# Twelve context projection units and the context norm moved into the convolution stage, all convolution taps on VectorE

## The reference, cut to what matters

```python
# first layer of the first block
u = h @ w_in + b_in                      # 1024 -> 2048
u = u[..., :D] * sigmoid(u[..., D:])     # GLU
u = causal_dwconv(u, dw, dw_b)           # depthwise, 31 taps over positions
u = silu(layer_norm(u, ln_g, ln_b))
y = u @ w_out + b_out

# second block: x is the stream, ctx a second input of 256 positions
mod  = silu(c)     @ ada_w + ada_b       # 6 x 1024, shift and scale of the stream
modc = silu(c_ctx) @ ada_w + ada_b       # only its shift sh1c and scale sc1c are used
u  = modulate(rmsnorm(x,   norm1_g), sh1,  sc1)
uc = modulate(rmsnorm(ctx, norm1_g), sh1c, sc1c)
pl, pc = split(u @ w_in_2), split(uc @ w_in_2)
# of pc: keys, values, gates of the mLSTM, keys and values of the diff attention
```

## Time and profile before

| what | value |
|---|---|
| median of 3 runs | 2381.61 us (2378.51 to 2382.83) |
| span of the profiled execution | 2380.3 us (it has no other time of its own) |
| mean granted TensorE clock | 0.994 |
| PE busy | 2316.2 us, 97% |
| DVE busy, ACT busy | 769.2 us, 423.7 us |
| DMA | 611.40 MB, 65% of the 16 engines' span |

### The profile page before, as it was taken

The page is one execution under the profiler, slowest core; times in us unless marked ns, Lnnn a source line. Parts: engine busy times, 40 slices in busy tenths (PEclk is TensorE's granted clock), DMA queues, the critical chain, the costliest instruction groups (busy, mean ns, idle before and its releaser), DMA issues.

```text
span 2380.3 us, 31802 instructions
## 1 busy us (share of the span) xinstructions
PE 2316.2 (97%) x13124; PEld 1756.2 (74%) x13124; DVE 769.2 (32%) x1881; ACT 423.7 (18%) x1035; POOL 0.2 (0%) x4
## 2 busy tenths in 40 slices
PE   9999999999999999999999999999999999998998
PEld 7888888888888888888887787555555555554555
DVE  7834374210435421100355823222222222221222
ACT  4332102010242211100024402111111111111111
POOL 0000000000000000000000000000000000000000
PEclk9999999999999999999999999999999999999999
DMA  7134476655324444234332377999999999999997
GB/s 268 40 138 157 145 291 238 230 214 192 107 89 142 155 146 142 71 123 134 86 120 87 140 276 287 404 426 427 429 427 428 427 428 427 429 427 427 427 427 297
DMA packets 61048, 611.40 MB, mean 257 GB/s; under 512 B 7016, under 2 KB 8424, under 8 KB 10896
## 3 DMA queue, kind: packets, MB, share of 16 engines
q1 hardware_dynamic: 60944, 609.93, 65.1%
HBM read 606.74 MB, written 1.06 MB: 255 GB/s over the span
## 4 chain that ended last, share of the span: by engine, by line
PE 81%; DMA 10%; DVE 7%; issue 1%; ACT 0%; DVEq 0%; SPq 0%; ACTq 0%
PE bank L645 28%; PE bank L1197 16%; PE bank L642 8%; DMA ring<-in_experts 6%; PE bank L1234 5%; PE bank L733 5%; DMA arena<-in_experts 4%; PE bank L659 3%; DVE arena L1868 3%; PE bank L634 2%; PE bank L1188 2%; PE bank L1156 1%; PE bank L1144 1%; PE bank L744 1%; PE bank L764 1%
## 5 line engine op out<-in xcount | busy, mean ns | idle before, releaser
L645 PE MATMUL bank<-arena,ring 128*128 128x256 f32 x3264 | 709.9, 380 | 0.0
L645 PEld LDWEIGHTS bank<-arena,ring 128*128 128x128 f32 x3264 | 620.8, 190 | 84.4
L2300 DVE TENSOR_SCALAR arena<-bank 128x256 f32<-128x256 f32 x64 | 27.1, 424 | 673.9 <-PE bank L1197 673.9
L1197 PE MATMUL bank<-ring,arena 128*64 128x256 f32 x2048 | 235.2, 384 | 9.0 <-DMA ring<-in_experts 6.7
L1197 PE MATMUL bank<-arena 128*64 128x256 f32 x2048 | 231.5, 380 | 10.5 <-DMA arena<-in_experts 10.3
L1197 PEld LDWEIGHTS bank<-ring,arena 128*64 128x64 f32 x2048 | 143.6, 138 | 115.6 <-issue 33.3
L1197 PEld LDWEIGHTS bank<-arena 128*64 128x64 f32 x2048 | 144.9, 137 | 98.6 <-DMA arena<-in_experts 17.2
L642 PE MATMUL bank<-ring,arena 128*128 128x256 f32 x896 | 194.0, 379 | 1.0 <-issue 1.0
L642 PEld LDWEIGHTS bank<-ring,arena 128*128 128x128 f32 x896 | 170.1, 190 | 24.4 <-issue 1.4
L733 PE MATMUL bank<-arena,ring 128*128 128x256 f32 x576 | 124.6, 379 | 0.0
L1625 ACT ACTIVATE arena<-arena 128x256 f32<-128x256 f32 x64 | 26.7, 416 | 533.9 <-DVE arena L2300 533.9
(11 more groups left out here) (306 smaller groups left out, 1907.5 us busy)
## 6 DMA issues: line engine op xcount, KB each, us to landing
arena<-in_experts SPq DMA_DIRECT2D x96, 2048.0 KB, 31.1
ring<-in_dense SPq DMA_DIRECT2D x185, 1024.0 KB, 4.9
ring<-in_experts SPq DMA_DIRECT2D x87, 2048.0 KB, 29.5
ring<-in_experts SPq DMA_DIRECT2D x16, 1024.0 KB, 31.4
ring<-arena SPq DMA_DIRECT2D x16, 128.0 KB, 5.8
con<-in_con SPq DMA_DIRECT2D x1, 1248.0 KB, 12.2
X<-in_x SPq DMA_DIRECT2D x2, 512.0 KB, 5.8
ring<-in_dense SPq DMA_DIRECT2D x2, 512.0 KB, 7.4
```

Source lines behind the costliest of these rows:

```text
L645: ins = nc.tensor.matmul(o, w[:, k, j * P:(j + 1) * P], src[:, k, :], start=(k == 0), stop=(k == KT - 1))
L1197: ins = nc.tensor.matmul(o, XGT[:, k, e * CAP:(e + 1) * CAP], w[:, k, :], start=False, stop=(k == KT - 1), skip_group_check=True)
```

## The change

- A stage `early` of 12 slabs and 12 units stands between `cm_in` and `cm_out`. Its slabs are copies of those of mv, dv and dk: each is now read twice, once for the context and once for the stream.
- The context norm and its modulation (eight slabs, read again for it into places of their own) run beside `cm_in`, on DVE in the middle of `conv(0)`.
- The results, and the normed context, are written to DRAM (`park`, 4 x 1 MB) and fetched back before `ffn1_in` slab 1 and before dk.
- All 31 taps of all eight tiles are on DVE; the diagonal matrices are gone, and the filler matmuls ahead of `cm_out`, in whose place half an early unit stands.
- mv, dk and dv have four units each; the wait for the read-out of dk is gone.

The core of the diff, cut:

```diff
-    ("cm_in", 8, 8), ("cm_out", 4, 4),
+    ("cm_in", 8, 8), ("early", EARLY, EARLY), ("cm_out", 4, 4),
...
-    ("mk", 2, 4), ("mq", 2, 2), ("mv", 4, 8),
-    ("dq", 4, 4), ("dk", 4, 8), ("dv", 4, 8),
+    ("mk", 2, 4), ("mq", 2, 2), ("mv", 4, 4),
+    ("dq", 4, 4), ("dk", 4, 4), ("dv", 4, 4),
...  (SP, ahead of slab g)
+                    sp.dma_start(CT, d_ctx).then_inc(sem("ctx_in"), 16)                       # g == 2
+                    sp.dma_start(CSR[:, 1, :], d_cond[:, D:2 * D]).then_inc(sem("ctx_in"), 16)
+                for i in ((), (0, 1), (2,), (3, 4), (5,), (6, 7))[g - 2] if 2 <= g < 8 else ():
+                    if i >= CTX_PLACES:
+                        sp.wait_ge(sem("ada_ctx"), 2 * (i - CTX_PLACES) + 2)
+                    sp.dma_start(ADA_C[i % CTX_PLACES], d_dense[SLAB_AT["ada", i]])...
+                if g == SLAB_AT["early", 0] + RING + 1:
+                    sp.wait_ge(sem("nc_h"), before("nc_h") + KT)
+                    park(3, UC)
+                for b in range(3):
+                    if g == SLAB_AT["early", 0] + 4 * b + 4 + RING:
+                        for u in range(3):
+                            unit_half(sp, FIRST_UNIT["early"] + 4 * b + 1 + u, 2)
+                        park(b, STAGED[b])
                 if g == SLAB_AT["ffn1_in", 1]:
                     sp.wait_ge(sem("att_out"), HEADS)
-                    sp.dma_start(CT, d_ctx).then_inc(sem("ctx_in"), 16)
+                    sp.wait_ge(sem("parked"), 4 * 16)
+                    sp.dma_start(UC, tiles(d_park[3], KT)).then_inc(sem("parked_back"), 16)
+                    sp.dma_start(DV[:, 0:2, :], tiles(d_park[1], 2)).then_inc(sem("parked_back"), 16)
+                    sp.dma_start(DK[:, :, 0:T], tiles(d_park[2], KT)).then_inc(sem("parked_back"), 16)
...  (PE)
-            conv_taps(5, banks[WORK + 3][:, 0:T], TAPS - PE_TAPS, 0)
-            conv_taps(6, banks[WORK + 1][:, 0:T], 0, PE_TAPS)
+            pe.wait_ge(sem("nc_h"), before("nc_h") + KT)
+            for n in range(7):
+                early(n)
             for c in range(4):
                 channel_sum(c)
-            conv_taps(7, banks[WORK + 2][:, 0:T], 0, PE_TAPS + TAPS)
-            for c in range(4, KT):
+            for n in range(7, EARLY - 2):
+                early(n)
+            for c in range(4, 6):
+                channel_sum(c)
+            early(EARLY - 2)
+            early(EARLY - 1, (0,))
+            for c in range(6, KT):
                 ins = channel_sum(c)
             ins.then_inc(sem("ln_mean"), 1)
             stat("ln", 1, mean)
-            stage("cm_out", H, "ln_h", busy=6)
+            early(EARLY - 1, (1,))
+            stage("cm_out", H, "ln_h")
...
-            units_read(pe, "dk")
             pe.wait_ge(sem("rt"), 1)
-            for i in range(8):
-                product(FIRST_UNIT["dv"] + i, SLAB_AT["dv", i // 2], (UC, H)[i % 2], True)
+            stage("dv", H, token_major=True)
...  (ACT)
             root("n0", 0)
+            act.wait_ge(sem("ctx_in"), 32)
+            nc.scalar.activation(CSR[:, 1, :], CSR[:, 1, :], ACT.Silu).then_inc(sem("silu_ctx_done_by_act"), 1)
+            square("nc", lambda c: CT[:, c, :])
             act.wait_ge(sem("par_in"), 16)
             for j in range(8):
+                if j == 3:
+                    root("nc", 1)
+                if j == 7:
+                    shifted("nc", 1, 0, UC)
...  (DVE)
+            def context():
+                dve.wait_ge(sem("ada_ctx"), 2 * CTX_ADA)
+                gains(1)
+                modulated("nc", rstd("nc", 1), CT, lambda c: GS1[:, c, 1:2], UC)
...
             raw_unit(0)
             normed("n0", factor, lambda c: ("mix_pre", c))
+            presum("nc")
             dve.wait_ge(sem("par_in"), 16)
             glu(0)
             raw_unit(1)
             glu(1)
-            conv(0)
+            beside = {k + 1: [(ada_ctx, (k,))] for k in range(CTX_ADA)}
+            beside[CTX_ADA + 2] = [(context, ())]
+            conv(0, beside)
             glu(2)
             glu(3)
-            conv(2, between={4: (4, 5), 14: (6,), 22: (7,)})
-            conv(4, own=(TAPS, TAPS - PE_TAPS))
-            dve.wait_ge(sem("conv_pe"), 1)
-            V.tensor_tensor(U[:, 5, :], U[:, 5, :], banks[WORK + 3][:, 0:T], ALU.add).then_inc(sem("conv"), 1)
+            conv(2, {4: [(glu, (4,)), (glu, (5,))], 14: [(glu, (6,))], 22: [(glu, (7,))]})
+            conv(4)
+            conv(6)
```

More of the change, by code:

```diff
@@ L460, in build, with early_to @@
                 if name in ("mq", "dq"):
[L461 to L468, removed]
+                    dst = [to[:, 2 * i + j, :] for j in range(2)]
+                elif name == "dk":
+                    dst = [to[:, 2 * i + j, T:2 * T] for j in range(2)]
+                else:
+                    dst = [to[:, 2 + j, i * T:(i + 1) * T] for j in range(2)]
+                second.append((FIRST_UNIT[name] + i, dst))
+        def early_to(n, j):
+            b, i = n // 4, n % 4
+            if b < 2:
+                return tiles(STAGED[b], 2)[:, j, i * T:(i + 1) * T]
+            return tiles(STAGED[b], KT)[:, 2 * i + j, :]
         def kvq(i, j):
@@ L841, in _ @@
             stage("cm_in", XG, first=1, count=1)
[L842 to L851, removed]
+            stage("cm_in", H, "n0_h", first=2, count=1)
@@ L853, in channel_sum @@
+            presummed("nc")
+            stage("cm_in", H, first=3, count=5)
             def channel_sum(c):
[L855 to L858, removed]
+                pe.wait_ge(sem("conv"), c + 1)
                 return nc.tensor.matmul(banks[WORK][:, 0:T], mean, U[:, c, :], start=(c == 0), stop=(c == KT - 1))
-            conv_taps(5, banks[WORK + 3][:, 0:T], TAPS - PE_TAPS, 0)
@@ L862, in _, with early @@
-            conv_taps(6, banks[WORK + 1][:, 0:T], 0, PE_TAPS)
+            def early(n, halves=(0, 1)):
+                u, g = FIRST_UNIT["early"] + n, SLAB_AT["early", n]
+                w = slab(g).rearrange("p (k n) -> p k n", k=KT)
+                if halves[0] == 0:
+                    slab_loaded(pe, g)
+                    unit_half(pe, u - UNIT_BANKS, 2)
+                for j in halves:
+                    for k in range(KT):
+                        if n < 8:
+                            ins = nc.tensor.matmul(half_of(u, j), UC[:, k, j * P:(j + 1) * P], w[:, k, :],
+                                                   start=(k == 0), stop=(k == KT - 1))
+                        else:
+                            ins = nc.tensor.matmul(half_of(u, j), w[:, k, j * P:(j + 1) * P], UC[:, k, :],
+                                                   start=(k == 0), stop=(k == KT - 1))
+                if halves[-1]:
+                    ins.then_inc(sem(f"unit{u % UNIT_BANKS}"), 1)
@@ L890, in _ @@
             presummed("n7")
-            stage("ffn1_in", H, first=1, count=10)
-            presummed("nc", 0)
-            stage("ffn1_in", H, first=11, count=11)
+            stage("ffn1_in", H, first=1, count=21)
             ffn_out(1, "n8")
[L896 to L903, removed]
+            pe.wait_ge(sem("parked_back"), 48)
             product(FIRST_UNIT["mk"], SLAB_AT["mk", 0], UC)
@@ L926, in _ @@
             ins.then_inc(sem("cumf_turn"), 1)
-            two("mv", True)
+            stage("mv", H, token_major=True)
             pe.wait_ge(sem("gate_steps"), 3)
@@ L1466, in _ @@
             root("n7", 1)
[L1467 to L1486 removed]
+            ffn_in(1)
             root_table("n8")
@@ L2359 @@
     }
+    weights["early"] = np.concatenate([weights["mv"], weights["dv"], weights["dk"]])
     for i in range(2):
```

168 lines of the change are left out of this document (82 added, 86 removed).

## The result

| | us |
|---|---|
| changed kernel, median of 4 runs | 2353.36 (2351.0 to 2356.95) |
| kernel before, beside it | 2381.86 (2378.51 to 2382.83) |
| ratio | 0.9882, 95% interval 0.987 to 0.9894 |
| profiled execution: own time, span | 2351.0, 2349.2 |

The account below looks back on a forecast made before the run. TensorE was taken as the bound, with VectorE setting the convolution stage and the weight stream the experts. Terms 51.2 - 83.0 - 0.4 - 1.0 + 1.5 = -31.7 us took span 2380.3 to 2348.6, time 2350; range 2343 to 2362.

Parts of the forecast that it names:

- (a) to (c): VectorE's chain in the convolution stage: conv starts at 29.1, conv(0) ends at 76.8, the last tap at 152.2 us.
- (a): VectorE before the first tap: the presum of context squares ahead of glu(0) makes conv start 2.7 us later.
- (f): DMA: 28 MB more, with modulation slabs queued behind waits, parking and fetches, all priced as free.
- (d): TensorE in the convolution stage: idles 3.7 us before sum 6; cm_out starts at 160.9, 51.2 us later.
- (g): TensorE's clock falls to half after the new idle in the convolution stage: +1.5 us, bounds 0 and 4.
- (e): mLSTM projections: -83.0, -0.4 and -1.0 us; k's rotation keeps about 5 us of cover, any excess paid one for one.
- The first: Convolution stage fully VectorE-bound and longer than priced: up to 12 us more, about 2362; chance 0.12.
- The second: mLSTM stage: k's turn and rotation end after dv, m_scores waits 3 to 15 us, say 2358; chance 0.08.
- The third: Convolution stage PE-bound, DVE ending by 148: no idle or clock fall, 5.2 us less, 2345; chance 0.07.
- Slab supply: Slabs of mv, dk and dv arrive slower than PE takes them: 33 us lost, or even 2409; chance 0.03.
- the unmoved expert stream: Expert stage at the end: its weight stream starts by something that does not move, nothing gained, 2381; chance 0.03.

Follow-up runs that it names:

- e0: The changed kernel itself, run once more without any edit: 2353.99 us.
- e2: Changed kernel with the modulation products three taps later in conv(0) and the context norm at tap 13 instead of 10: 2354.08 us.
- e1: Changed kernel with 13 filler matmuls on TensorE in the idle before channel sums 6 and 7: 2351.99 us.
- e5: Changed kernel with the 32 narrow gate matmuls placed two by two behind wide matmuls of the last mk unit, instead of in a block: 2349.84 us.
- e9: Changed kernel with 30 idle VectorE operations inside the rotation of k, holding it up by 13.7 us: 2361.69 us.
- e4: Changed kernel with later modulation products, the context squares' adds spread between taps, and the first tap of tiles 2 to 7 on ScalarE: 2351.0 us.
- e8: Changed kernel with the first eight taps of channel tiles 6 and 7 given back to TensorE: 2353.4 us.
- e3: Kernel before with only the tap part of the change, all taps on VectorE and context work as before: 2411.61 us.
- e6: Changed kernel with the wait for the read-out of all dk units put back ahead of dv: 2356.64 us, a single time.
- e7: Changed kernel with the edits of e4 and e5 together, plus three filler matmuls before channel sums 6 and 7: 2342.83 us.

## Why the prediction was right

- *Where the gain is.* Cm_out later by 55.3, the mLSTM projections shorter by 84.6, the expert stage earlier with them. 2353.36 beside the forecast 2350, within the range.
- *(a) to (c), VectorE's chain.* The last tap but one ended at 153.1 for 151.8. That this is so near is in part luck, as two errors cancel. Conv started at 27.25, not 29.1: 1.4 us of it because this execution's head was earlier (in e0, with a later head, 29.26), and 0.4 because (a) was priced too long. And the taps lost 2.7 us to the slabs of (f). The context norm took 5.4 us, tap pairs 24.4, as priced, and without the slab waits, in e2, the stretch from the first tap to sum 6 is 123.2 us, where the prediction has 122.7.
- *(f), the step that was wrong in kind:* I had the modulation slabs land 2.5 us ahead of their use. The sixth and seventh came late by 0.7 and 1.8: issued at 33.4 and 36.5, behind what was already on a queue that moved 418 to 424 GB/s, they could not be used before 44.1 and 49.1, 10.7 and 12.6 us later. The conclusion "free" fell, the price (1.1 to 2.7, e2) was inside the range.
- *(d), the idle.* 6.2 us for 3.7: PE was 1.2 us earlier (146.9 for 148.1), DVE 1.3 later.
- *(g), the clock:* the mechanism right, the term mis-sized: +1.5 forecast, 2.55 by e1 and 4.0 in e0. The Trainium skill, "TensorE: Matmul & The Clock Gate", Part 1 with its section on HAM oscillation, says that an idle gap drops the clock to half and that sustained work brings it back. The windows at 150 (0.50) and 160 (1.00) and e1 agree. What I missed is a second place: the block of narrow gate matmuls, where PE is busy and the clock falls all the same. It was there in the kernel before, which I had not looked at. By the stretch that e5 shortens it costs 3.3 to 6.6 us, depending on the execution.
- *(e), the cover behind dv.* The rotation ended 4.0 us before dv for "about 5". That the excess past this point would be paid one for one is refuted by e9: the read-out behind it decides, later.
- *Rivals.* The first (a longer DVE chain) came in part, by the slabs, under 3 us. The second did not come. The third is what e4 and e8 reach only by edits. Slab supply and the unmoved expert stream are refuted by the first gate half and the end moving 29 to 31 us.
- *The span is 31.1 us shorter, the stages above give 29.3.* 1.4 of the rest is one fall of the clock at 1340 that this execution did not have after the same idle; e1, e3, e4, e5, e6 and e7 had it, e0, e2, e8 and e9 not. 0.4 is behind it, in the gates and experts, and stays open. So does the rest of the spread from 2351 to 2357: other executions than the profiled one have no trace. That the span comes within 0.6 us of the forecast is in part luck: this execution is the fastest of the four, its head is 1.4 us earlier than that of the kernel before, and it lacks the fall at 1340. The span of e0, the same code, is 27.8 us shorter than before.

## What to carry to other kernels

Where two engines share a stage, work given to the bound one is paid in full (e3), and work put on the idle one beside it is free up to the point where their ends meet (e4, e8): write down both sequences to their ends before moving either. Fill what idle remains, or the clock takes part of the gain back (e1), and look for narrow matmuls in blocks: a busy engine can stand at half clock (e0), and mixing them between wide ones saved 4.1 us here (e5).

## What the runs showed of the hardware that I had not expected

- A block of 64 records of 128x16 matmuls, PE busy 100%, was followed by a granted clock of 0.50 for 7 to 14 us in all ten profiled executions that have it; the same matmuls in twos between wide ones left it at 1.00 (e5, e7).
- The same idle of 2.2 us between two attention steps, at 1340 in the kernel before, brought the clock to half in seven executions (before, e1, e3, e4, e5, e6, e7) and not in five (the changed kernel, e0, e2, e8, e9). Before sums 6 and 7 an idle of 1.54 us, with 0.96 us more behind them, brought it to half in e4, while 1.74 and 0.96 at the same place in the kernel before did not.
- The head of the kernel, up to the first unit's norm sum, lay between 13.6 and 17.3 us in the ten profiled executions of the changed kernel and its variants, with nothing changed ahead of it.
